# Products and result of an 8x8 forward substitution kept in PSUM (chunked gated delta rule, one Trainium2 core)

## The chip, the cores and the metric

The kernel runs on one core of one Trainium2 chip. The metric is device time in microseconds for one execution. Five engines work side by side, each through its own list of instructions in order, and wait for each other by semaphores: TensorE (PE: matmuls, with its weight loads shown as PEld), VectorE (DVE), ScalarE (ACT), GpSimd (POOL) and SyncE (SP, which here only issues DMAs). On-chip data lie in SBUF, or in PSUM, the eight banks that matmuls write.

## The reference, cut to what matters

One encoder layer in fp32 over 2048 + 256 tokens of width 1024: RMSNorm, one input projection, two mixers side by side (a gated convolution and a bidirectional gated DeltaNet), an output projection, then a mixture of experts and a last RMSNorm. The change lies in the DeltaNet, for which each of 4 heads and each direction solves a unit lower triangular system per chunk of tokens:

```python
lmat = jnp.where(strict, jnp.einsum('bhnid,bhnjd->bhnij', kb, k) * decay, 0.0)
tinv = lax.linalg.triangular_solve(lmat + eye, jnp.broadcast_to(eye, lmat.shape),
                                   left_side=True, lower=True, unit_diagonal=True)
w = jnp.einsum('bhnij,bhnjd->bhnid', tinv, kb * jnp.exp(gc)[..., None])
u = jnp.einsum('bhnij,bhnjd->bhnid', tinv, v * beta[..., None])
...
def step(s, xs):                       # scan over the chunks
    v_new = un - jnp.einsum('bhid,bhde->bhie', wn, s)
    o = jnp.einsum('bhid,bhde->bhie', qd, s) + jnp.einsum('bhij,bhje->bhie', qkn, v_new)
    s = s * jnp.exp(gl)[..., None, None] + jnp.einsum('bhid,bhie->bhde', kd, v_new)
```

## The kernel before, in words

The program is a sequence of stages, each a block of its own: `normalise`, `project` (the input projection, with the convolutions), `decays`, `delta`, `output`, `route`, `experts`, `combine`. Nothing of one stage runs beside the next but what has been issued before.

`delta` goes through 18 chunks of 128 tokens. Chunk `a` is taken forward in lane 0 and backward in lane 1 (`lanes`, one set of tiles `L[d]` and semaphores `E[d]` each), with four heads side by side in every 128x512 tile. `run` writes out the first three and the last three chunks and the step that empties the pipeline, and puts the twelve between them in a loop of two per turn. In the step of chunk `a` the inverse of that chunk is made while the scan of chunk `c` = `a` - 1 is finished. There is no scheduler: every engine's order is the order of the code.

In one step the work follows this chain.

- PE makes k k^T into bank `A[0]` of each lane, DVE multiplies it by the decays (`lt`, L1132), POOL masks out the 8x8 blocks on the diagonal (`near`, L861), DVE folds them (L1135, L1140), and one matmul of PE per step (L990) puts the entries that each row needs for its own block in `local`, which is `L[0]["A"][0]`.
- `solve` on DVE (L1096 to L1111) does the forward substitution for both lanes and all heads at once: seven times a product `step8` = column of `local` times column of `X8` (L1105; one operand in PSUM, one in SBUF, result in SBUF) and a subtraction `X8` - `step8` (L1108 the first, L1110 the rest; both operands in SBUF). Each waits on `base` for the one ahead of it, so there are 14 increments per chunk.
- For each lane DVE spreads `X8` over the block diagonal of `R` by a product with the mask `block8` (L1150; both operands in SBUF) and transposes it into `Tm` (`turn`, L1117).
- Four levels of `inverse` then double the block size, 8 to 128: PE multiplies `M` (POOL's masked parts of `lt`, one per level, L867) by `Tm` into `A[1]` (`X_ready`), ACT copies it to `X` (L945), PE multiplies `X` by `R` into `A[0]` (`dR_ready`), DVE subtracts it from `R` (L1155) and transposes again. At the last level PE transposes (L963) and ACT copies.

PE's order in a step is set in its `step` (L1045 to L1057): the four products of chunk `a`, `s(0)` of the scan, the `local` matmul, `s(1)`, `s(2)`, `s(3)` of the scan (the last is `kdec` by `vn`), then level 0 of `inverse`, whose first matmul waits for `T_set`, the transpose of `R`. POOL's order in a step is `near` for both lanes, `M` of levels 0 and 1, `keT` and `qdT` for both lanes (L876, L877), `M` of levels 2 and 3, then `masked` for the next chunk (L852); each is an operation on 128x512 elements with two operands in SBUF. POOL waits for nothing that `solve` makes.

The lines that the change touches are the allocation of `step8` (L784), the products and subtractions of `solve` (L1105 to L1111) and the operand of L1150.

Of the kernel before, what the change touches and what calls it, by code (L numbers as in the profile page):

```python
# [29 lines left out]
P = 128  # L30
# [6 lines left out]
HEADS = 4  # L37
# [25 lines left out]
def bcast(ap, n, axis):  # L63

    v = ap.unsqueeze(axis)
    shape = list(v.shape)
    shape[axis] = n
    return v.broadcast_to(shape)
# [685 lines left out]
def delta(nc, k, gates, gc_rows, feat, O):  # L754
# [12 lines left out]
    with ExitStack() as ctx:  # L767
        b = Bufs(nc, ctx, "delta_")
        L = []
# [11 lines left out]
            L.append(v)  # L781

        spread = b.sb("spread", [P, 2, HEADS, 8, 8])
        step8, X8 = b.sb("step8", [P, 2 * HEADS, 8]), b.sb("X8", [P, 2 * HEADS, 8])  # L784
        sems = ("loaded0 loaded1 row_loaded0 row_loaded1 masked gates_set kk qk kturned vturned eg_set dec_set lt_set near_set blk_set spread_set qkT_set keT_set "
                "qdT_set M_set kdec_set vtok_set R_set Tturned T_set T_last_set X_ready X_set dR_ready kS_ready rv_set Tv_ready vn_set "
                "o_ready o_added kv_ready S_set").split()
# [1 line left out]
        local_ready, base, begun8 = b.sem("local_ready"), b.sem("base_steps"), b.sem("X8_begun")  # L789
# [2 lines left out]
        NL = LEVELS - BASE  # L792

        local = L[0]["A"][0]

        def tile(d, s):

            if isinstance(s, int) and s >= LT_TILES:
                return s if d == 0 else NT - 1 - (s - LT_TILES)
            return s if d == 0 else s * -1 + (LT_TILES - 1)  # L800
# [261 lines left out]
        def _(dve):  # L1062
            def residual(c, r):
                for d, v, e in lanes:
                    dve.wait_ge(e["vtok_set"], c + 1)
                    dve.wait_ge(e["kS_ready"], c + 1)
                    dve.tensor_tensor(v["rv"][:, :, :], v["vtok"][r][:, :, :], v["B"][0][:, :, :], ALU.subtract).then_inc(e["rv_set"], 1)

            def advance(d, c, r):
                v, e = L[d], E[d]  # L1070
                dve.wait_ge(e["kv_ready"], c + 1)
                dve.wait_ge(e["S_set"], state(c))
                for h in range(HEADS):
                    m = dve.scalar_tensor_tensor(out=v["S"][:, h, :], in0=v["S"][:, h, :], scalar=v["gs"][r][:, 8 + h:9 + h],
                                                 in1=v["B"][1][:, h], op0=ALU.mult, op1=ALU.add)
                m.then_inc(e["S_set"], 1)

            def emit(d, c):

                v, e = L[d], E[d]  # L1080
                dve.wait_ge(e["o_ready"], c + 1)
                wait_if_any(dve, E[1 - d]["o_added"], c)
                out = O[:, bass.ds(tile(d, c), 1), :].rearrange("p a (h c) -> p (a h) c", h=HEADS)
                dve.tensor_tensor(out, v["B"][0][:, :, :], out, ALU.add).then_inc(e["o_added"], 1)

            def clear_state(c):
                for d, v, e in lanes:
                    if c:

                        dve.wait_ge(e["S_set"], c + 1)  # L1090
                    dve.memset(v["S"][:, :, :], 0.0).then_inc(e["S_set"], 1)

            def local_view(d):
                return slice(None, None, -1) if d else slice(None)

            def solve(a):  # L1096

                whole = local[:, :, :].rearrange("p h c -> p (h c)").rearrange("p (m j r) -> p m j r", j=8, r=8)
                unit = k["unit8"][:, :, :]
                dve.wait_ge(local_ready, a + 1)  # L1100
                for j in range(7):
                    w = 7 - j
                    if j:
                        dve.wait_ge(base, a * 14 + 2 * j)
                    dve.tensor_tensor(step8[:, :, 0:w], whole[:, :, j, j + 1:8], bcast(X8[:, :, j], w, 2), ALU.mult).then_inc(base, 1)  # L1105
                    dve.wait_ge(base, a * 14 + (2 * j + 1))
                    if j == 0:
                        dve.tensor_tensor(X8[:, :, 1:8], unit[:, :, 1:8], step8[:, :, 0:w], ALU.subtract).then_inc(base, 1)  # L1108
                    else:
                        dve.tensor_tensor(X8[:, :, j + 1:8], X8[:, :, j + 1:8], step8[:, :, 0:w], ALU.subtract).then_inc(base, 1)  # L1110
                dve.wait_ge(base, a * 14 + 14)  # L1111

            def turn(v, e, r, a, l):

                dve.wait_ge(e["R_set"], a * (NL + 1) + (l + 1))
                flat = [x.rearrange("p h c -> p (h c)") for x in (v["Tm"][:, :, :], v["R"][r][:, :, :])]
                dve.transpose(*flat).then_inc(e["T_set"], 1)  # L1117

            def step(a, c, r):
                if a is None:  # L1120
                    residual(c, 1 - r)
                    for d in range(2):
                        advance(d, c, 1 - r)
                        emit(d, c)
                    return
                if isinstance(c, int) and c == LT_TILES:
                    clear_state(c)
                for d, v, e in lanes:
                    dve.wait_ge(e["dec_set"], a + 1)
                    dve.wait_ge(e["kk"], a + 1)  # L1130
                    wait_if_any(dve, e["M_set"], a * NL)
                    dve.tensor_tensor(v["lt"][:, :, :], v["A"][0][:, :, :], v["dec"][:, :, :], ALU.mult).then_inc(e["lt_set"], 1)  # L1132
                for d, v, e in lanes:
                    dve.wait_ge(e["near_set"], a + 1)
                    dve.tensor_reduce(v["blk"][:, :, local_view(d)], v["near"][:, :, :].rearrange("p h (b r) -> p h r b", r=8),  # L1135
                                      AX.X, ALU.add).then_inc(e["blk_set"], 1)
                    dve.wait_ge(e["blk_set"], a + 1)
                    wait_if_any(dve, local_ready, a)
                    one = k["unit8"][:, d * HEADS:(d + 1) * HEADS, :]
                    dve.tensor_tensor(spread[:, d], bcast(v["blk"][:, :, :], 8, 2), bcast(one, 8, 3), ALU.mult).then_inc(e["spread_set"], 1)  # L1140
                for d, v, e in lanes:
                    dve.wait_ge(e["qk"], a + 1)
                    dve.tensor_tensor(v["qkT"][r][:, :, :], v["A"][1][:, :, :], v["dec"][:, :, :], ALU.mult).then_inc(e["qkT_set"], 1)
                if c is not None:
                    residual(c, 1 - r)
                solve(a)
                for d, v, e in lanes:
                    part = bcast(X8[:, d * HEADS:(d + 1) * HEADS, local_view(d)], P // 8, 2)
                    mask = bcast(k["block8"][:, :].rearrange("p (b r) -> p b r", r=8), HEADS, 1)
                    dve.tensor_tensor(v["R"][r][:, :, :].rearrange("p h (b r) -> p h b r", r=8), part, mask, ALU.mult).then_inc(e["R_set"], 1)  # L1150
                    turn(v, e, r, a, 0)
                for l in range(NL):
                    for d, v, e in lanes:
                        dve.wait_ge(e["dR_ready"], a * NL + (l + 1))
                        dve.tensor_tensor(v["R"][r][:, :, :], v["R"][r][:, :, :], v["A"][0][:, :, :], ALU.subtract).then_inc(e["R_set"], 1)  # L1155
                        if l < NL - 2:
                            turn(v, e, r, a, l + 1)
                    if c is not None and l < 2:
                        advance(l, c, 1 - r)
                        emit(l, c)  # L1160

            clear_state(0)
            dve.tensor_copy(X8[:, :, 0:1], k["unit8"][:, :, 0:1])
            run(dve, step)


# [18 lines left out]
def wait_if_any(eng, sem, value):  # L1185

    if not isinstance(value, int) or value > 0:
        eng.wait_ge(sem, value)
# [901 lines left out]
```

## Time and profile before

| | us |
|---|---|
| time, median of 3 runs (3218.67 to 3228.97) | 3221.87 |
| the profiled execution's own time | 3223.99 |
| its span, first to last instruction | 3222.4 |
| PE busy | 2732.1 (85%) |
| DVE busy | 2039.0 (63%) |
| POOL busy | 1128.5 (35%) |
| ACT busy | 1011.8 (31%) |
| mean granted clock of TensorE, as a share of full speed | 0.924 |

The `delta` stage lies at about 926 to 1671 us of the span. A busy share is a mean over stages with different limits, so the change is read in that stage alone, in a chunk of it. The time of one execution differs from the span by what lies around the span, here 1.6 us.

### The profile page before, as it was taken

The page shows a single profiled execution, that of the slowest core. Times are in us where ns is not written, and L with a number is a line of the kernel's source. Part 1 is how long each engine was busy: PE and PEld are TensorE (multiplying, and loading weights), DVE is VectorE, ACT ScalarE, POOL GpSimd, SP SyncE. Part 2 cuts the span into 40 slices and gives each one's busy share as a digit, 9 for nine tenths or more (in the row PEclk, how much of TensorE's full clock was granted, in tenths as well). Part 3 has the DMA queues.
Part 4 walks back from the last instruction along what each step waited for, and adds up shares of the span by engine and source line. Part 5 has one row for each costly group of instructions (what it writes and reads, how often), then busy time and mean ns, then how long its engine had stood idle before and what let it go on. Part 6 is the DMA issues. An engine that isn't in the chain of part 4 may idle for free. (4 is left out here: it accounts for less than half of the span.)

```text
span 3222.4 us, 45930 instructions
## 1 busy us (share of the span) xinstructions
PE 2732.1 (85%) x15152; PEld 2417.5 (75%) x15153; DVE 2039.0 (63%) x2191; ACT 1011.8 (31%) x2067; POOL 1128.5 (35%) x841
## 2 busy tenths in 40 slices
PE   5999999999858888888888995698899999999840
PEld 4998989989747777777776884576787888778730
DVE  5465564655537777777763335879678576877827
ACT  5152351523523333333323221122222323222223
POOL 4110110101035555555522221444354354435424
PEclk9999999999979999999998997799999999999975
DMA  4011120111121111111005441688567565757639
GB/s 151 27 59 41 48 67 29 58 39 48 42 83 53 53 52 52 52 52 52 27 13 173 138 154 52 240 304 317 205 251 272 208 236 215 286 208 293 235 142 359
DMA packets 228387, 433.96 MB, mean 135 GB/s; under 512 B 15065, under 2 KB 104393, under 8 KB 228170
## 3 DMA queue, kind: packets, MB, share of 16 engines
q1 hardware_dynamic: 207336, 349.86, 31.2%
q0 software_dynamic: 13328, 55.06, 4.7%
q10 hardware_dynamic: 7634, 27.79, 2.1%
q8 instruction: 64, 1.05, 0.1%
q14 instruction: 25, 0.20, 0.0%
HBM read 352.75 MB, written 87.25 MB: 137 GB/s over the span
## 5 line engine op out<-in xcount | busy, mean ns | idle before, releaser
L468 PE MATMUL project_proj<-hT_high,project_w_high 128*128 128x412 f32 (+3 forms) x1392 | 496.3, 357 | 28.0 <-issue 10.4
L468 PE MATMUL project_proj<-hT_low,project_w_high 128*128 128x412 f32 (+3 forms) x1392 | 474.9, 341 | 0.0
L468 PE MATMUL project_proj<-hT_high,project_w_low 128*128 128x412 f32 (+3 forms) x1392 | 474.8, 341 | 0.0
L1682 DVE TENSOR_TENSOR experts_w_low<-experts_w_whole,experts_w_high 128x2048 fp32r<-128x2048 f32 x128 | 355.6, 2778 | 4.4
L1776 PE MATMUL experts_h<-experts_w_high,experts_xT_high 128*128 x848 | 340.5, 401 | 18.8 <-DVE experts_w_low L1682 11.8
L1776 PE MATMUL experts_h<-experts_w_low,experts_xT_high 128*128 x848 | 338.9, 400 | 0.0
L1776 PE MATMUL experts_h<-experts_w_high,experts_xT_low 128*128 x848 | 337.5, 398 | 0.0
L1680 DVE CAST experts_w_high<-experts_w_whole 128x2048 fp32r<-128x2048 f32 x128 | 191.6, 1497 | 168.4 <-DMA experts_w_whole<-in_w_dram 168.3
L468 PEld LDWEIGHTS project_proj<-hT_high,project_w_high 128*128 128x128 f32 (+1 forms) x1392 | 261.4, 188 | 45.1 <-issue 31.6
L958 PE MATMUL delta_prep<-delta_Tm,delta_M 128*128 128x128 f32 x1152 | 185.1, 319 | 119.5 <-DVE delta_Tm L1117 116.9
L468 PEld LDWEIGHTS project_proj<-hT_low,project_w_high 128*128 128x128 f32 (+1 forms) x1392 | 261.3, 188 | 14.4 <-issue 9.8
L468 PEld LDWEIGHTS project_proj<-hT_high,project_w_low 128*128 128x128 f32 (+1 forms) x1392 | 260.9, 187 | 5.2 <-issue 0.7
L958 PEld LDWEIGHTS delta_prep<-delta_Tm,delta_M 128*128 128x128 f32 x1152 | 166.3, 226 | 131.0 <-issue 75.9
L445 POOL CAST project_w_high<-project_w_whole 128x1024 fp32r<-128x1024 f32 x28 | 30.3, 1084 | 639.2 <-DMA project_w_whole<-in_w_tiles_dram 639.2
L1797 PE MATMUL experts_ye<-experts_w_high,experts_gT_high 128*128 128x512 f32 x424 | 178.2, 420 | 55.1 <-DVE experts_w_low L1696 42.1
L1716 POOL COPY experts_ix<-idx 128x1 int32 (+1 forms) x55 | 28.7, 521 | 530.6 <-PE experts_xg_turned L1769 516.6
L1776 PEld LDWEIGHTS experts_h<-experts_w_high,experts_xT_high 128*128 128x128 f32 x848 | 161.3, 190 | 58.5 <-issue 21.3
L945 ACT ACTIVATE delta_X<-delta_prep 128x512 f32<-128x512 f32 x144 | 86.0, 597 | 375.9 <-PE delta_prep L958 375.9
L636 DVE RECIPROCAL project_norms<-project_norms 128x409 f32<-128x409 f32 (+1 forms) x72 | 183.8, 2553 | 24.9 <-ACT project_norms L560 24.4
L1155 DVE TENSOR_TENSOR delta_R<-delta_R,delta_prep 128x512 f32<-128x512 f32 x144 | 97.7, 679 | 160.1 <-PE delta_prep L958 160.1
L867 POOL TENSOR_TENSOR delta_M<-delta_lt,lvl 128x512 f32<-128x512 f32 x144 | 195.2, 1387 | 0.0
L1776 PEld LDWEIGHTS experts_h<-experts_w_low,experts_xT_high 128*128 128x128 f32 x848 | 161.6, 191 | 36.5
(282 smaller groups left out, 5814.3 us busy)
## 6 DMA issues: line engine op xcount, KB each, us to landing
experts_w_whole<-in_w_dram SPq DMA_DIRECT2D x128, 1024.0 KB, 10.1
experts_w_whole<-in_w_dram SPq DMA_DIRECT2D x32, 2048.0 KB, 18.6
delta_qkv<-feat SPq DMA_DIRECT2D x36, 768.0 KB, 4.9
y_rows<-experts_yout ACTq DMA_DIRECT2D x53, 512.0 KB
project_w_whole<-in_w_tiles_dram SPq DMA_DIRECT2D x28, 512.0 KB, 4.3
feat<-project_out SPq DMA_DIRECT2D x48, 205.0 KB, 1.9
normalise_x<-in_x_dram SPq DMA_DIRECT2D x18, 512.0 KB, 3.2
delta_row<-gc_rows SPq DMA_DIRECT2D x36, 256.0 KB, 3.3
```

The lines of the kernel that those rows point to most:

```text
L445: pool.tensor_copy(high[s][:, :, :], whole[s][:, :, :]).then_inc(w_high, 1)
L468: r = pe.matmul(dst, w[s][:, kt, 0:m], x[:, kt, lo:hi], start=kt == 0 and i == 0, stop=kt == KD - 1 and i == 2)
L636: dve.reciprocal(r, r).then_inc(inverted, 1)
L867: pool.tensor_tensor(v["M"][:, l], v["lt"][:, :, :], bcast(k["lvl"][:, d, l, :], HEADS, 1), ALU.mult).then_inc(e["M_set"], 1)
L945: act.activation(v["X"][:, :, :], v["A"][1][:, :, :], ACT.Copy).then_inc(e["X_set"], 1)
L958: m = pe.matmul(out[:, h], lhsT(h), rhs(h), start=start and h == 0, stop=stop, skip_group_check=True)
L1155: dve.tensor_tensor(v["R"][r][:, :, :], v["R"][r][:, :, :], v["A"][0][:, :, :], ALU.subtract).then_inc(e["R_set"], 1)
L1680: dve.tensor_copy(high, loaded).then_inc(e["w_high_set"], 1)
L1682: m = dve.tensor_tensor(low, loaded, high.bitcast(F32), ALU.subtract)
L1716: pool.tensor_copy(ix[p][:, :], idx[:, bass.ds(blk, 1)]).then_inc(e["ix_set"], 1)
L1776: m = pe.matmul(out[:, :], x[p][:, kt, :], w, start=kt == 0 and i == 0, stop=kt == KD - 1 and i == 2)
L1797: m = pe.matmul(Y[n][:, :], g[:, c, :], w, start=c == 0 and i == 0, stop=c == FF // P - 1 and i == 2)
```

## The change

The product tile `step8` moves from SBUF to PSUM, to the first 64 columns of head 0 of `L[1]["A"][0]`, the bank of lane 1 in which k k^T stood and which its levels write again later. The running solution `X8` stays in SBUF. When the 14 operations are done, one copy on DVE puts it into the first 64 columns of head 1 of the same bank (`solved8`), and L1150 (L1153 in the changed file) reads it there instead of `X8`. The copy has its own increment of `base`, so there are 15 per chunk.

```diff
-        step8, X8 = b.sb("step8", [P, 2 * HEADS, 8]), b.sb("X8", [P, 2 * HEADS, 8])
+        X8 = b.sb("X8", [P, 2 * HEADS, 8])
...
         local = L[0]["A"][0]
+        step8, solved8 = (L[1]["A"][0][:, n, 0:16 * HEADS].rearrange("p (m r) -> p m r", r=8) for n in range(2))
...
                 for j in range(7):
                     w = 7 - j
                     if j:
-                        dve.wait_ge(base, a * 14 + 2 * j)
+                        dve.wait_ge(base, a * 15 + 2 * j)
                     dve.tensor_tensor(step8[:, :, 0:w], whole[:, :, j, j + 1:8], bcast(X8[:, :, j], w, 2), ALU.mult).then_inc(base, 1)
-                    dve.wait_ge(base, a * 14 + (2 * j + 1))
+                    dve.wait_ge(base, a * 15 + (2 * j + 1))
...
-                dve.wait_ge(base, a * 14 + 14)
+                dve.wait_ge(base, a * 15 + 14)
+                dve.tensor_copy(solved8[:, :, :], X8[:, :, :]).then_inc(base, 1)
+                dve.wait_ge(base, a * 15 + 15)
...
-                    part = bcast(X8[:, d * HEADS:(d + 1) * HEADS, local_view(d)], P // 8, 2)
+                    part = bcast(solved8[:, d * HEADS:(d + 1) * HEADS, local_view(d)], P // 8, 2)
```

On DVE, the end of `solve` in a step and what follows stood thus before (`delta_step` is `step8` in SBUF):

```order
L1105 TENSOR_TENSOR delta_step<-delta_prep,delta_X 128x8
L1110 TENSOR_TENSOR delta_X<-delta_X,delta_step 128x8
L1150 TENSOR_TENSOR delta_R_1<-delta_X,block 128x512
L1117 STREAM_TRANSPOSE delta_Tm<-delta_R_1 128x512
L1150 TENSOR_TENSOR delta_R_1<-delta_X,block 128x512
L1117 STREAM_TRANSPOSE delta_Tm<-delta_R_1 128x512
```

In the changed kernel the same place reads as follows (`delta_prep` is any of the PSUM banks `A`):

```order
L1106 TENSOR_TENSOR delta_prep<-delta_prep,delta_X 128x8
L1111 TENSOR_TENSOR delta_X<-delta_X,delta_prep 128x8
L1113 COPY delta_prep<-delta_X 128x64
L1153 TENSOR_TENSOR delta_R_1<-delta_prep,block 128x512
L1120 STREAM_TRANSPOSE delta_Tm<-delta_R_1 128x512
L1153 TENSOR_TENSOR delta_R_1<-delta_prep,block 128x512
L1120 STREAM_TRANSPOSE delta_Tm<-delta_R_1 128x512
```

One COPY of 128x64 comes in behind the last subtraction, once per step. No other instruction moves on DVE, and the orders of PE, POOL, ACT and SP are those of before.

## Rows read from the trace of the kernel before

**Rows 1.** Waits in the delta stage, 930 to 1660 us: total, times, longest.

```profile
PE delta_prep L958 <- DVE delta_Tm L1117: 116.7, 26, 11.0
```

**Rows 2.** Timeline of a chunk in the loop and the next, PE: start, us, instructions, [idle before].

```profile
1316.69 1.95 PE L958 MATMUL delta_scan<-delta_vn,delta_kdec 128*128 128x128 f32 x16
...
1324.80 3.75 PE L958 MATMUL delta_prep<-delta_Tm,delta_M 128*128 128x128 f32 x16 [6.16 <-DVE delta_Tm L1117]
...
1331.39 2.38 PE L958 MATMUL delta_prep<-delta_Tm,delta_M 128*128 128x128 f32 x16
...
1336.35 2.32 PE L958 MATMUL delta_prep<-delta_Tm,delta_M 128*128 128x128 f32 x16
...
1365.74 3.75 PE L958 MATMUL delta_prep<-delta_Tm,delta_M 128*128 128x128 f32 x16 [6.20 <-DVE delta_Tm L1117]
```

**Rows 3.** Timeline of the same chunk, DVE.

```profile
1313.41 0.21 DVE L1105 TENSOR_TENSOR delta_step<-delta_prep,delta_X 128x56 f32<-128x56 f32 x1
1313.66 1.12 DVE L1108 TENSOR_TENSOR delta_X<-unit,delta_step 128x56 f32<-128x56 f32 x1
1314.81 0.21 DVE L1105 TENSOR_TENSOR delta_step<-delta_prep,delta_X 128x48 f32<-128x48 f32 x1
1315.05 0.95 DVE L1110 TENSOR_TENSOR delta_X<-delta_X,delta_step 128x48 f32<-128x48 f32 x1
...
1322.11 1.70 DVE L1150 TENSOR_TENSOR delta_R<-delta_X,block 128x512 f32<-128x512 f32 x1
1323.85 0.71 DVE L1117 STREAM_TRANSPOSE delta_Tm<-delta_R 128x512 f32<-128x512 f32 x1
```

**Rows 4.** Timeline of the same chunk, POOL.

```profile
1314.66 1.28 POOL L876 TENSOR_TENSOR delta_keT<-delta_qkv,delta_eg 128x512 f32<-128x512 f32 x1
1315.88 1.28 POOL L877 TENSOR_TENSOR delta_qdT<-delta_qkv,delta_eg 128x512 f32<-128x512 f32 x1
...
1319.55 5.38 POOL L867 TENSOR_TENSOR delta_M<-delta_lt,lvl 128x512 f32<-128x512 f32 x4
1324.89 2.93 POOL L852 TENSOR_TENSOR delta_masked<-delta_row,neg 128x512 f32<-128x512 f32 x2
1347.67 2.51 POOL L861 TENSOR_TENSOR delta_near<-delta_lt,strict 128x512 f32<-128x512 f32 x2 [19.85 <-DVE delta_lt L1132]
```

**Rows 5.** Groups of DVE instructions by shape: busy us, mean ns, idle before.

```profile
L1155 DVE TENSOR_TENSOR delta_R<-delta_R,delta_prep 128x512 f32<-128x512 f32 x144 | 97.7, 679 | 160.1 <-PE delta_prep L958 160.1
L1105 DVE TENSOR_TENSOR delta_step<-delta_prep,delta_X 128x56 f32<-128x56 f32 x18 | 3.8, 212 | 0.0
L1105 DVE TENSOR_TENSOR delta_step<-delta_prep,delta_X 128x8 f32<-128x8 f32 x18 | 3.1, 173 | 0.6
L1140 DVE TENSOR_TENSOR delta_spread<-delta_blk,unit 128x256 f32<-128x256 f32 x36 | 15.5, 430 | 1.2
```

**Rows 6.** The small copies on DVE, each alone: duration in ns, when, shape.

```profile
L1163 DVE COPY delta_X<-unit x1: 111/111/111, 927.9 to 927.9; 128x8 f32<-128x8 f32 x1
L731 DVE COPY decays_ab_gc<-decays_pg x2: 233/234/234, 922.7 to 923.5; 128x72 f32<-128x72 f32 x2
```

**Rows 7.** Stretches: length, PE, PEld, DVE, ACT, POOL busy, granted clock, DMA share.

```profile
1307.00:1318.64 11.64, 11.64 (x95) 10.55 (x93) 10.66 (x18) 4.35 (x12) 11.64 (x10) 1.00 0.01 3
1324.80:1328.13 3.33, 3.33 (x16) 3.33 (x16) 1.39 (x2) 0.60 (x1) 3.03 (x3) 0.50 0.00 0
1290.37:1295.27 4.90, 4.81 (x42) 4.62 (x41) 4.29 (x10) 1.20 (x2) 0.00 (x0) 1.00 0.00 0
```

**Rows 8.** Timeline of a written-out chunk (second of the stage) and of the first.

```profile
996.61 3.78 PE L958 MATMUL delta_prep<-delta_Tm,delta_M 128*128 128x128 f32 x16 [5.89 <-DVE delta_Tm L1117]
1003.46 1.06 PE L958 MATMUL delta_prep<-delta_Tm,delta_M 128*128 128x128 f32 x8
...
955.84 3.78 PE L958 MATMUL delta_prep<-delta_Tm,delta_M 128*128 128x128 f32 x16 [11.04 <-DVE delta_Tm L1117]
...
944.83 0.22 DVE L1105 TENSOR_TENSOR delta_step<-delta_prep,delta_X 128x56 f32<-128x56 f32 x1
```

## The prediction

> **What bounds the kernel now.** I read the waits of the delta stage first, then one chunk of it on PE, DVE and POOL side by side, then the groups for durations and a few stretches for the granted clock. In the waits, PE's longest is for `Tm`, the transposed block diagonal that closes the substitution: 116.7 us in all [rows 1]. The chunk shows where. PE ends the `kdec` by `vn` matmuls of the scan at 1318.64 (1316.69 + 1.95) and then stands idle for 6.16 us until level 0 of the inverse starts at 1324.80 [rows 2]. Before that it had worked without a gap: 11.64 of 11.64 us [rows 7]. What it waits for is one chain on DVE: the substitution starts at 1313.41, the first spread `R` at 1322.11, its transpose ends at 1324.56 (1323.85 + 0.71), and PE follows 0.24 us later [rows 2, 3]. So in this stretch DVE's chain ends last, and its length from 1313.41 to PE's start is 11.39 us.
>
> Why is that chain long? A product of 56 elements with one operand in PSUM takes 0.21 us; a subtraction of 48 elements with both in SBUF takes 0.95, and a `R` of 512 elements with both in SBUF 1.70 [rows 3], where the `R` update of 512 elements with one in PSUM has 0.679 [rows 5]. Size doesn't explain it; POOL does. The subtraction at 1315.05 ends at 1316.00, just behind POOL's `keT` (1314.66 + 1.28 = 1315.94), which started before it; and POOL's operations follow each other every 1.22 us (1314.66 to 1315.88), so each subtraction seems to wait out one of them [rows 3, 4]. A two-operand SBUF instruction that is not held in this way is in the trace too: L1140 has 256 elements in 0.430 [rows 5]. I read this as DVE's second SBUF operand waiting for the POOL instruction that is running.
>
> **The change part by part.** The change leaves one SBUF operand in each instruction of the chain, so I price each as an unheld one.
>
> Seven products write to PSUM instead of SBUF. They go from 212 ns at 56 elements to 173 at 8 [rows 5]; about 0.192 each in the mean, 7 x 0.192 = 1.34 us. The trace has no DVE instruction that writes PSUM. From below, it costs nothing extra; a gain is excluded, since the same elements pass. From above, I let the part of an instruction that does not depend on its size, about 0.165 us (the 8 elements of the 173 ns take few of them: (212 - 173)/48 = 0.8 ns each), come twice. I take nothing, nearest to the row of the same instruction, and keep + 0.165 for the range.
>
> Seven subtractions read `step8` in PSUM and `X8` in SBUF. Nearest is the product itself, the same shape with the same two kinds of operands: again 1.34 us. Now they and the pauses take 8.70 us less these products (1313.41 to 1322.11), so this is where nearly all of the gain lies.
>
> One copy of 64 elements comes in, with its wait: nearest is the copy of 72 elements at 0.233 [rows 6]; from below the copy of 8 at 0.111, from above a held instruction at 0.95 [rows 3]. I take 0.23.
>
> The pauses between dependent instructions stay: 1313.66 - 1313.62 = 0.04 in rows 3, mean about 0.035, for 15 instructions 0.5 us. No increment of `base` moves but the added one, and nothing but `R` is queued behind it.
>
> `R` of the first lane: 0.68 as the 512-element update with one PSUM operand [rows 5], 0.73 with its pause, instead of 1.70. Transpose and PE's reaction stay at 0.71 and 0.24.
>
> Sum from the start of the substitution to PE's level 0: 1.34 + 1.34 + 0.23 + 0.5 + 0.73 + 0.71 + 0.24 = 5.1 us instead of 11.39, so `Tm` comes 6.3 us earlier, at 1318.5. PE is then done with the scan at 1318.64, so its own order ends last and the gain is the idle time, 6.16 us, with next to nothing to spare: whatever the PSUM accesses cost beyond this is paid in full. Twelve chunks in the loop have this pattern. Five of the six written out have 5.89 us of idle time [rows 8]; the first chunk has no scan beside it, so there the chain alone counts: 955.84 - 944.83 = 11.01 less 5.1 is 5.9. Together 12 x 6.16 + 5 x 5.89 + 5.9 = 109.3 us.
>
> A second term hangs on the first. After the idle time the granted clock is 0.50 (1.2 GHz) through the first matmuls of level 0, where it is 1.00 (2.4 GHz) before the idle time and in level 1 of the chunk ahead [rows 7]. Level 0 therefore takes 1331.39 - 1324.80 = 6.59 us to the start of level 1, and level 1 to level 2, the same instructions, 1336.35 - 1331.39 = 4.96 [rows 2]; in the written-out chunks it is 1003.46 - 996.61 = 6.85 [rows 8]. Without the idle time PE comes out of 11 us of gapless work at 1.00, so I count 12 x 1.63 + 5 x 1.89 = 29.0 us. In the first chunk PE still waits 5 us, so I count nothing there.
>
> What is late next: POOL's `M` of level 2. POOL doesn't wait for the substitution, so it makes it at the times of now, from 1319.55, the first two of four by 1322.3 and all by 1324.9 [rows 4]; PE, starting level 0 at 1318.6, asks for level 2 at 1318.6 + 2 x 4.96 = 1328.5. `masked` is done at 1327.8, and the decays that need it come at the end of level 3. POOL then has 19.85 us without work now [rows 4] and would have 12. The second lane's `R` and transpose end 1.4 us behind the first's, at 1319.7, while PE works on the first lane. The other DVE work in the levels has one SBUF operand already, so POOL's shift against it costs nothing.
>
> Against this sum stands the Trainium skill, in "Perfetto Trace Analysis", section "Optimizing Scalar/DVE Operations": about 60 ns of access overhead per DVE operation on SBUF and about 125 on PSUM. Here 56 elements with a PSUM source take 212 ns where L1140's 430 for 256 SBUF elements, less 200 for the difference at 1 ns each ((679 - 430)/256), would make 230: no surcharge for reading. If the page's 65 ns came on top for each of the eight instructions that now write PSUM, an estimate by it is 0.5 us per chunk, 9 us in all.
>
> Total: 109.3 + 29.0 = 138.3 us. From the profiled execution's own 3223.99 this leaves 3085.7; the median of the runs, 3221.87, is 2.1 us lower. I say 3085.
>
> **Rivals.**
>
> *PSUM as a destination costs time.* For it: no row shows such an instruction, and there is no slack. Against: reading PSUM shows no price. With 0.165 more for each of the seven products and the copy, 8 x 0.165 x 18 = 24 us come back: 3109. If instead only the copy is held by POOL like a subtraction now, 0.72 x 18 = 13: 3098. The Trainium skill ("VectorE: DVE Perf Modes", section "Mode 2×_2P — use both read ports for one tensor") has a one-source copy use the second port only with source and destination in SBUF; by that rule the copy isn't held, which takes from this second form.
>
> *The clock doesn't come back.* Level 0 stays at 0.50 for another reason than the idle time. For it: the clock is granted by something that the trace doesn't show. Against: in each chunk it is 1.00 up to the idle time. Time: 3085 + 29 = 3114.
>
> *The change doesn't do what it says.* The subtractions are held whatever their operands, and the copy adds 0.27 with its pause, 18 x 0.27 = 5 us, on the chain that ends last: 3229. Against: the products, with one SBUF operand, are never held (173 to 212 ns in the means) while the same POOL instructions run.
>
> *Slower.* PSUM writes of DVE are held themselves, by TensorE's writes into other banks, which fill the whole substitution now. With h for each of eight such instructions, the chain is 5.1 + 8h, and from h = 0.78 the kernel is slower. At h = 1.0, what `R` is held today (1.70 - 0.68), it is 8.0 - 6.3 = 1.7 us per chunk, 31 in all: 3255. Against: DVE reads PSUM beside the same matmuls and shows no hold.
>
> **How the numbers follow.** Forecast 0.67, with 3076 to 3096 as its own range (the 5 us that the runs of before spread downwards; the page's estimate upwards); PSUM destinations 0.15; clock 0.11; no effect 0.04; slower 0.03. The range of 3074 to 3114 takes in the first three. Under 0.3% (10 us) a measurement of this kernel can't be told from no change: faster 0.93, same 0.04, slower 0.03.
>
> **What would show it.** In the changed profile the subtractions are at about 0.17 to 0.21 us and `R` at 0.68 while POOL runs; the copy at 0.23; PE's wait for `Tm` falls from 116.7 us to under 15, most of it in the first chunk; the stretch from level 0 to level 1 is about 5 us at a granted clock of 1.00; chunks follow every 33 us, where level 0 now starts every 41 (1324.80 to 1365.74) [rows 2]. It is wrong if the products or the copy grow past 0.3 us, if PE still waits more than 1 us per chunk before level 0, or if another wait, `M` of level 2 above all, stands in the levels.

## The result, and the profile after

| | before | changed |
|---|---|---|
| first set of runs, median | 3220.27 us (4 runs, 3217.71 to 3228.97) | 3073.8 us (4 runs, 3070.73 to 3075.78) |
| second set, median | 3218.46 us (14 runs, 3208.05 to 3226.68) | 3075.66 us (5 runs, 3071.51 to 3080.87) |
| ratio, first set | | 0.954 [0.9519, 0.956] |
| ratio, second set | | 0.955 [0.953, 0.9569] |
| profiled execution, and its span | 3223.99, 3222.4 | 3070.73, 3069.1 |
| first `masked` to last `kdec` matmul, in the profile | 930.2 to 1681.4: 751.2 | 922.4 to 1529.8: 607.4 |

The kernel is 4.5% faster. The forecast was 3085, its range 3074 to 3114: the first median lies 0.2 us under the range's low end, the second 1.7 us inside. On which side of the end a median falls is within the scatter of the runs; that the forecast was 9 to 11 us too high is not. The stage `delta` runs to 1681 us in the profile before, ten more than the 1671 given ahead of the prediction.

The wait that bounded the stage, in the waits of the changed kernel (930 to 1540 us; total, times, longest), against [rows 1]:

```profile
PE delta_prep L959 <- DVE delta_Tm L1120: 6.5, 5, 5.0
```

It fell from 116.7 us to 6.5, of which 5.0 are the first chunk's. A chunk of the loop on PE, and level 0 of the next, against [rows 2]:

```profile
1237.47 1.95 PE L959 MATMUL delta_scan<-delta_vn,delta_kdec 128*128 128x128 f32 x16
...
1239.32 2.29 PE L959 MATMUL delta_prep<-delta_Tm,delta_M 128*128 128x128 f32 x16
...
1244.19 2.32 PE L959 MATMUL delta_prep<-delta_Tm,delta_M 128*128 128x128 f32 x16
...
1249.09 2.32 PE L959 MATMUL delta_prep<-delta_Tm,delta_M 128*128 128x128 f32 x16
...
1272.19 2.29 PE L959 MATMUL delta_prep<-delta_Tm,delta_M 128*128 128x128 f32 x16
```

Level 0 starts at 1239.32, where the modelled end of the scan's matmuls is 1239.42: no idle time is left. Level 0 to level 1 takes 4.87 us in place of 6.59, and the next chunk's level 0 comes 32.9 us later in place of 40.9. The same chunk on DVE, against [rows 3]:

```profile
1234.20 0.21 DVE L1106 TENSOR_TENSOR delta_prep<-delta_prep,delta_X 128x56 f32<-128x56 f32 x1
1234.45 0.21 DVE L1109 TENSOR_TENSOR delta_X<-unit,delta_prep 128x56 f32<-128x56 f32 x1
1234.69 0.22 DVE L1106 TENSOR_TENSOR delta_prep<-delta_prep,delta_X 128x48 f32<-128x48 f32 x1
1234.94 0.20 DVE L1111 TENSOR_TENSOR delta_X<-delta_X,delta_prep 128x48 f32<-128x48 f32 x1
...
1237.38 0.23 DVE L1113 COPY delta_prep<-delta_X 128x64 f32<-128x64 f32 x1
1237.64 0.69 DVE L1153 TENSOR_TENSOR delta_R<-delta_prep,block 128x512 f32<-128x512 f32 x1
1238.37 0.71 DVE L1120 STREAM_TRANSPOSE delta_Tm<-delta_R 128x512 f32<-128x512 f32 x1
```

The first subtraction went from 1.12 us to 0.21, `R` from 1.70 to 0.69. From the first product to level 0 it is 5.12 us in place of 11.39. POOL did not get out of the way: it works without a pause from 1227.57 to 1247.79. Rows of it in the same chunk, against [rows 4]:

```profile
1235.45 1.27 POOL L877 TENSOR_TENSOR delta_keT<-delta_qkv,delta_eg 128x512 f32<-128x512 f32 x1
...
1240.38 4.95 POOL L868 TENSOR_TENSOR delta_M<-delta_lt,lvl 128x512 f32<-128x512 f32 x4
1245.30 2.49 POOL L853 TENSOR_TENSOR delta_masked<-delta_row,neg 128x512 f32<-128x512 f32 x2
1260.41 2.51 POOL L862 TENSOR_TENSOR delta_near<-delta_lt,strict 128x512 f32<-128x512 f32 x2 [12.62 <-DVE delta_lt L1135]
```

Its four `M` of levels 2 and 3 even run a little faster (4.95 us in place of 5.38), since DVE's `R` no longer comes between. The groups of the chain, against [rows 5, 6]:

```profile
L1153 DVE TENSOR_TENSOR delta_R<-delta_prep,block 128x512 f32<-128x512 f32 x36 | 24.2, 672 | 0.6
L1113 DVE COPY delta_prep<-delta_X 128x64 f32<-128x64 f32 x18 | 4.1, 228 | 0.6
L1106 DVE TENSOR_TENSOR delta_prep<-delta_prep,delta_X 128x56 f32<-128x56 f32 x18 | 3.9, 215 | 0.0
L1106 DVE TENSOR_TENSOR delta_prep<-delta_prep,delta_X 128x8 f32<-128x8 f32 x18 | 3.1, 174 | 0.6
L1111 DVE TENSOR_TENSOR delta_X<-delta_X,delta_prep 128x48 f32<-128x48 f32 x18 | 3.7, 204 | 0.6
```

Every duration of the sum came out within 12 ns: products 215 to 174 (212 to 173 with SBUF as destination), subtractions 204 at 48 elements, copy 228, `R` 672. The granted clock through the first matmuls of level 0 (third number from the end, 1.00), against the 0.50 of [rows 7]:

```profile
1239.32:1242.65 3.33, 3.33 (x28) 3.14 (x28) 1.15 (x3) 1.19 (x2) 3.33 (x3) 1.00 1.01 280
```

### The profile page after: what moved, and what is told of

The parts are those of the page before. It is cut to its first block and busy times, and to the rows that moved or that the text cites. A ratio compares the mean times of both kernels' runs of the same rounds, so it can differ in the third digit from the quotient of the medians.

```text
span 3069.1 us, 45960 instructions
## 1 busy us (share of the span) xinstructions
PE 2689.6 (88%) x15152; PEld 2375.8 (77%) x15153; DVE 1919.5 (63%) x2209; ACT 1011.7 (33%) x2067; POOL 1105.3 (36%) x841
## 5 line engine op out<-in xcount | busy, mean ns | idle before, releaser
L1685 DVE TENSOR_TENSOR experts_w_low<-experts_w_whole,experts_w_high 128x2048 fp32r<-128x2048 f32 x128 | 349.3, 2729 | 4.4
L468 PEld LDWEIGHTS project_proj<-hT_high,project_w_high 128*128 128x128 f32 (+1 forms) x1392 | 260.5, 187 | 44.3 <-issue 30.4
L868 POOL TENSOR_TENSOR delta_M<-delta_lt,lvl 128x512 f32<-128x512 f32 x144 | 187.3, 1331 | 0.0
L1779 PEld LDWEIGHTS experts_h<-experts_w_high,experts_xT_low 128*128 128x128 f32 x848 | 160.0, 189 | 35.0
L1699 DVE TENSOR_TENSOR experts_w_low<-experts_w_whole,experts_w_high 128x2048 fp32r<-128x2048 f32 x64 | 175.9, 2748 | 2.2
L1800 PE MATMUL experts_ye<-experts_w_low,experts_gT_high 128*128 x424 | 176.4, 416 | 0.0
```

Of the source, the lines that this page charges most:

```text
L468: r = pe.matmul(dst, w[s][:, kt, 0:m], x[:, kt, lo:hi], start=kt == 0 and i == 0, stop=kt == KD - 1 and i == 2)
L868: pool.tensor_tensor(v["M"][:, l], v["lt"][:, :, :], bcast(k["lvl"][:, d, l, :], HEADS, 1), ALU.mult).then_inc(e["M_set"], 1)
L1685: m = dve.tensor_tensor(low, loaded, high.bitcast(F32), ALU.subtract)
L1699: m = dve.tensor_tensor(w2_low[:, p, cs], w2_whole[:, p, cs], w2_high[:, cs].bitcast(F32), ALU.subtract)
L1779: m = pe.matmul(out[:, :], x[p][:, kt, :], w, start=kt == 0 and i == 0, stop=kt == KD - 1 and i == 2)
L1800: m = pe.matmul(Y[n][:, :], g[:, c, :], w, start=c == 0 and i == 0, stop=c == FF // P - 1 and i == 2)
```

## The experiments

Two things were open: that POOL's running instruction, and nothing else about two SBUF operands, made the subtractions slow; and that the clock at level 0 came back because PE's idle time went. Three more questions were how the gain divides, whether there is slack, and what the 8 us are by which the stages ahead of `delta` ended earlier in the profile.

**The changed kernel again.**

> The changed kernel once more, timed against the kernel before in five rounds. Theory A (a DVE instruction with two SBUF operands waits out the POOL instruction that is running; with the operands in PSUM the chain of the substitution is short, and PE's own order comes next): the delta stage, from the first masked of POOL to the last kdec matmul, takes 606 us again, 144 less than before, and the time is 3069 to 3076. The rest of the gain of the first execution, about 8 us by which the stages ahead of delta ended earlier, is then a matter of the single execution: the last matmul of the projection, at 908.4 us in the first profile of before and at 900.7 in that of the changed kernel, comes anywhere between 898 and 911. Rival: the changed program makes the earlier stages faster every time; then the projection ends near 901 again and the ratio stays at or under 0.954.

Measured 3075.66 us, `delta` 608.0 us (928.6 to 1536.6), projection's last matmul at 906.7. Over the eleven profiles of this study that matmul, in code that no kernel here alters, came between 900.7 and 908.4, in no order with the change. The span outside `delta` was 2471.2 us both before and in this execution, and 2461.7 in the first of the changed kernel. So the gain of the change is the 143 to 144 us of `delta`; the rival falls. Why the stages outside `delta` differ by some us from one execution to the next stays open.

**Products in PSUM alone.** No copy, `R` from `X8` (the edit is shown against the changed kernel):

```diff
-                dve.wait_ge(base, a * 15 + 14)
-                dve.tensor_copy(solved8[:, :, :], X8[:, :, :]).then_inc(base, 1)
-                dve.wait_ge(base, a * 15 + 15)
+                dve.wait_ge(base, a * 14 + 14)
...
-                    part = bcast(solved8[:, d * HEADS:(d + 1) * HEADS, local_view(d)], P // 8, 2)
+                    part = bcast(X8[:, d * HEADS:(d + 1) * HEADS, local_view(d)], P // 8, 2)
```

> Products in PSUM, so that the subtractions have one SBUF operand; no copy, and R is made from X8 in SBUF as before (two SBUF operands). Theory A: the subtractions take 0.17 to 0.21 us, R of the first lane is held by whatever POOL runs, 0.7 to 1.7 us, on average some 0.5 above 0.68, against 0.26 saved on the copy. PE waits 0.1 to 0.7 us per chunk for Tm, the granted clock at level 0 is 1.00, time 3074 to 3086. Rival (the copy and R in PSUM carry much of the gain, or the clock drops again): PE waits 1 us or more per chunk, time above 3095.

Measured 3085.74 us, ratio 0.9582 [0.9562, 0.9602]; `delta` 616.9 us, 9 more than the changed kernel. DVE and POOL in a chunk:

```profile
1249.67 1.10 DVE L1151 TENSOR_TENSOR delta_R<-delta_X,block 128x512 f32<-128x512 f32 x1
...
1251.44 1.01 DVE L1151 TENSOR_TENSOR delta_R<-delta_X,block 128x512 f32<-128x512 f32 x1
```

```profile
1248.95 1.27 POOL L878 TENSOR_TENSOR delta_qdT<-delta_qkv,delta_eg 128x512 f32<-128x512 f32 x1
1250.18 1.72 POOL L877 TENSOR_TENSOR delta_keT<-delta_qkv,delta_eg 128x512 f32<-128x512 f32 x1
```

`R` is held until POOL's `qdT` ends at 1250.22, and then 0.55 us remain; POOL's `keT`, which starts beside it, takes 1.72 us in place of 1.27. The hold goes both ways. In the loop level 0 starts about 0.14 us later behind the `local` matmul than in the repeat, and lasts 5.23 us in place of 4.87, since PE waits 0.36 us in it for the second lane's `Tm`; these make up most of the 9 us that the copy and `R` in PSUM are worth of the 143.

**Copy and `R` in PSUM alone.** Products in SBUF as before, the copy and the changed L1150 kept.

> Products in SBUF as before, so the subtractions keep two SBUF operands; only the copy to PSUM is added and R reads it there. Theory A: subtractions 0.93 to 1.1 us as before, copy 0.23, R 0.67 in place of 1.70 in the first lane. The chain is 11.39 - 1.02 + 0.26 = 10.6 us, PE still waits about 5.4 us per chunk, and the granted clock at level 0 is still 0.50; 18 x 0.77 = 14 us gained, time about 3207 (3202 to 3212). Rival (half the gain or more is R's, or the clock comes back once the wait is a little shorter): under 3180.

Measured 3206.53 us, ratio 0.9965 [0.9952, 0.9977], `delta` 738.2 us, 13 less than before. Its level 0, on PE:

```profile
1313.67 3.75 PE L959 MATMUL delta_prep<-delta_Tm,delta_M 128*128 128x128 f32 x16 [5.44 <-DVE delta_Tm L1120]
```

The wait is 0.7 us shorter, and the first matmuls last 3.75 us, as at the low clock before. As expected; the gain is the subtractions', with the clock that follows from them.

**POOL's instructions made short.** The kernel before with `M`, `keT` and `qdT` made for one head of four (the others are zero); the `masked` for the next chunk stay whole. The edit of `M`, with `keT` and `qdT` likewise:

```diff
-                        pool.tensor_tensor(v["M"][:, l], v["lt"][:, :, :], bcast(k["lvl"][:, d, l, :], HEADS, 1),
+                        pool.tensor_tensor(v["M"][:, l, 0:1], v["lt"][:, 0:1, :], bcast(k["lvl"][:, d, l, :], 1, 1),
```

> The kernel before, with POOL's M, keT and qdT made for one of the four heads only (the other three stay zero), so that POOL's instructions beside the substitution have 128 elements instead of 512, some 0.35 to 0.45 us each instead of 1.27. DVE's instructions are those of before, all with two SBUF operands where they had them. Theory A: a subtraction waits out a shorter POOL instruction, so it takes 0.2 to 0.45 us instead of 0.95 while POOL still runs, and 0.17 to 0.21 once POOL has finished its M; the substitution takes 3.2 to 5 us instead of 8.7. Rival (two SBUF operands are slow by themselves, whatever POOL does): the subtractions stay at 0.93 to 1.1 us and the substitution at 8.7.

One substitution ran through all three states of POOL. POOL, then DVE:

```profile
1220.06 1.69 POOL L867 TENSOR_TENSOR delta_M<-delta_lt,lvl 128x128 f32<-128x128 f32 x4
1221.71 2.49 POOL L852 TENSOR_TENSOR delta_masked<-delta_row,neg 128x512 f32<-128x512 f32 x2
```

```profile
1220.67 0.33 DVE L1113 TENSOR_TENSOR delta_X<-unit,delta_step 128x56 f32<-128x56 f32 x1
...
1221.28 0.54 DVE L1115 TENSOR_TENSOR delta_X<-delta_X,delta_step 128x48 f32<-128x48 f32 x1
...
1222.09 0.95 DVE L1115 TENSOR_TENSOR delta_X<-delta_X,delta_step 128x40 f32<-128x40 f32 x1
...
1223.30 0.96 DVE L1115 TENSOR_TENSOR delta_X<-delta_X,delta_step 128x32 f32<-128x32 f32 x1
...
1224.51 0.18 DVE L1115 TENSOR_TENSOR delta_X<-delta_X,delta_step 128x24 f32<-128x24 f32 x1
...
1225.56 0.69 DVE L1155 TENSOR_TENSOR delta_R<-delta_X,block 128x512 f32<-128x512 f32 x1
```

Beside POOL's 128-element `M`, one every 0.41 us, the subtractions take 0.33 and 0.54 us; beside the two 512-element `masked`, 0.95 and 0.96; after POOL's last ends at 1224.20, 0.18, with both operands in SBUF as ever; and `R`, both operands in SBUF too, takes 0.69 us in place of 1.70. This settles the cause: not the operands' place by itself, but POOL's running instruction. The 512-element ones were the `masked`, which I had not counted on, so the values above 0.45 and the 5.13 us of the whole substitution were outside the expectation. The time of this one run, 3074.14 us, is no measure of the gain: `delta` took 634.8 us, 27 more than in the repeat, and the rest of the span 2437.7 us, 33 less than before; the later stages work on other values there, and why they end sooner is not shown.

**The copy five times.**

> The changed kernel with the copy made five times in a row, each waiting for the one ahead: four more of 0.265 us with their pauses on the chain, 1.06 us per chunk. Theory A with no slack left, as the prediction has it: PE waits about 1 us longer per chunk, 18 x 1.06 = 19 us, time about 3091 (3087 to 3094), clock at level 0 still 1.00. Rival (the chain ends well before PE's own order, so there is slack): under 3080. A third way: the longer wait lets the granted clock fall at level 0; then 1.6 to 1.9 us per chunk more, about 3120.

Measured 3098.79 us, ratio 0.9624 [0.9601, 0.9646]; `delta` 627.2 us, 19.2 more than in the repeat of the changed kernel. PE waits 0.95 us per chunk, and the matmuls of level 0 are at full clock:

```profile
1221.53 2.29 PE L959 MATMUL delta_prep<-delta_Tm,delta_M 128*128 128x128 f32 x16 [0.95 <-DVE delta_Tm L1121]
```

In the twelve chunks of the loop the four added copies delay level 0 by 1.05 us, all of what they take, so there the chain on DVE still ends last, without slack; in the five written out behind the first chunk they delay it by 0.84 to 0.91, so there PE's own order had ended some 0.2 us behind the chain. From the `local` matmul to level 0 the changed kernel takes 6.31 us in the loop and 6.22 in four of those five; an estimate from these is that shortening the chain further could still give about 0.1 us per chunk of the loop, 1 us in all. The median lies 5 us above the expectation's upper end, where the stage in the profile has the expected 19; the runs go from 3093.87 to 3105.32.

**PE kept busy, substitution as before.** Filling matmuls (identity by identity, into a bank that is free there) ahead of level 0, first 40, then 20, then 28:

```diff
                 s(3)
+                for d, v, e in lanes:
+                    pe.wait_ge(e["qkT_set"], a + 1)
+                for n in range(10):          # then 5, then 7
+                    by_heads(L[1]["A"][1], lambda h: k["ident"][:, :], lambda h: k["ident"][:, :])
                 for l in range(NL):
```

> The kernel before, with 40 matmuls of 128 columns (identity by identity, into a bank that is free there) put on PE behind the scan's kdec matmuls and ahead of level 0: about 4.6 us of the 6.16 us in which PE waits for Tm. The substitution is left as it was. Theory A with the second term of the prediction (the clock falls because PE is idle): the chain on DVE still ends last, PE waits some 1.5 us, the granted clock at level 0 is 1.00, level 0 to level 1 takes 4.9 us instead of 6.59, and 17 x 1.6 to 1.9 = 28 to 31 us are gained, time about 3190 (3186 to 3196). Rival (the low clock at level 0 has another reason): no gain, 3215 to 3225, granted clock 0.50 there.

Measured 3227.52 us, ratio 1.0027 [1.0017, 1.0037]: no gain, and `delta` 8.5 us longer. That was my sizing: each fp32 matmul is recorded as two instructions, so the filling took 8.9 us and delayed level 0. The time therefore decides nothing between the theories. The trace does: with no idle time left ahead of level 0, the clock there is 1.00 in all 17 chunks behind the first, and level 0 takes 4.53 us, with the substitution as slow as before.

> The kernel before with half as many filling matmuls on PE as in the run before it: 20 of 128 columns. In that run 40 were recorded as 80 instructions of 0.11 us each (fp32 takes two), 8.9 us from start to start in place of 4.6, so PE reached level 0 about 2.8 us after Tm was there, though the granted clock was 1.00 and level 0 to level 1 took 4.53 us. With 20 the filling takes 4.5 us of the 6.3 that PE waits. Theory A (the clock at level 0 follows from PE's idle time): PE waits about 1.6 us for Tm, clock 1.00 at level 0, level 0 to level 1 4.9 us in place of 6.59; 12 x 1.7 + 5 x 1.9 = 30 us gained, time about 3189 (3184 to 3194). Rival (what the changed kernel gained at level 0 came from the shorter R and transposes of the second lane and not from the clock): gain under 10 us.

Measured 3212.6 us, ratio 0.9966 [0.9951, 0.9982], `delta` 8.5 us shorter. The clock did not stay up throughout. Two chunks on PE, the first with the clock at 1.00, the second where it fell:

```profile
1273.85 1.13 PE L958 MATMUL delta_prep<-delta_Tm,delta_M 128*128 128x128 f32 x8 [1.71 <-DVE delta_Tm L1121]
1275.34 1.16 PE L958 MATMUL delta_prep<-delta_Tm,delta_M 128*128 128x128 f32 x8 [0.35 <-DVE delta_Tm L1121]
1279.07 2.32 PE L958 MATMUL delta_prep<-delta_Tm,delta_M 128*128 128x128 f32 x16
...
1313.43 1.13 PE L958 MATMUL delta_prep<-delta_Tm,delta_M 128*128 128x128 f32 x8 [1.72 <-DVE delta_Tm L1121]
1314.92 1.97 PE L958 MATMUL delta_prep<-delta_Tm,delta_M 128*128 128x128 f32 x8 [0.36 <-DVE delta_Tm L1121]
1320.22 1.01 PE L958 MATMUL delta_prep<-delta_Tm,delta_M 128*128 128x128 f32 x7
```

Level 0 to level 1 is 5.22 us in the first and 6.79 in the second; of the 17 chunks behind the first, 9 were of the second kind, with the same waits as the others (1.4 to 1.8 us, and 0.3 to 0.5 in the second lane's half). My expectation of 30 us failed.

> The kernel before with 28 filling matmuls on PE, between the 20 and the 40 of the two runs ahead of this one: 56 instructions of 0.1115 us are 6.2 us, which closes the 6.3 us that PE waits for Tm to about 0.1. With 20 it still waited 1.7 us and the clock fell all the same in 9 of 17 chunks, in the second lane's half of level 0. Theory A: with no idle time left the clock is 1.00 in level 0 of all chunks, level 0 to level 1 takes 5.2 us (6.59 before; the 0.35 that the changed kernel saves beyond this is the second lane's shorter R), the chain on DVE is not touched, so 17 x 1.4 = 24 us are gained, time 3192 to 3202. Rival: the clock falls in some chunks also without idle time, gain under 15 us.

Measured 3200.52 us, ratio 0.9937 [0.9923, 0.995], 20 us less than before, and 23.5 us less in `delta` of the profile (727.8). No chunk behind the first fell. Level 0 in one of them, on PE and in the clock:

```profile
1304.19 6.42 PE L958 MATMUL delta_prep<-ident 128*128 128x128 f32 x56
1310.55 1.13 PE L958 MATMUL delta_prep<-delta_Tm,delta_M 128*128 128x128 f32 x8
1312.04 1.16 PE L958 MATMUL delta_prep<-delta_Tm,delta_M 128*128 128x128 f32 x8 [0.36 <-DVE delta_Tm L1121]
...
1315.78 1.54 PE L958 MATMUL delta_prep<-delta_Tm,delta_M 128*128 128x128 f32 x9
```

```profile
1310.57:1315.80 5.23, 4.87 (x42) 4.68 (x42) 3.02 (x5) 1.20 (x2) 3.02 (x3) 1.00 0.00 0
```

With the substitution untouched and as slow as ever, level 0 takes 5.23 us in place of 6.6. The second term is real, and it hangs on PE's idle time.

> The kernel before with 20 filling matmuls as two runs ahead, but on data (kdec by kdec) in place of identity by identity, which is nearly all zeros. If the clock fell in 9 of 17 chunks there because of the 1.7 us that PE still waits, it falls in about as many here. Rival: it fell because multiplying zeros counts for less; then it is 1.00 in all chunks here and level 0 to level 1 takes 5.2 us in each.

One run, 3211.88 us: with data in place of zeros the clock fell in 11 of the 17 chunks. So zeros were not the reason.

## Why the prediction was right in its steps and short in its size

The mechanism held: the hold by POOL, its end, the return of the clock. What failed is the size, in two places: three terms of the sum were about 5 us too small together, and the base from which the sum was taken was about 4 us too high. Both erred the same way.

- *The hold by POOL, and its end with one operand in PSUM*: right, and shown by the run with POOL's short instructions. One reading beside it was not: L1140, taken as an instruction that is not held, had started ahead of POOL's and held POOL instead (its rows are in the last section).
- *PSUM as a destination costs nothing*: right but for a little. The seven products sum to 1.39 us in the repeat's profile where they took 1.345, 6 ns each. The estimate by "Perfetto Trace Analysis" of the Trainium skill, section "Optimizing Scalar/DVE Operations", 65 ns each, is ten times what the trace shows, and the measurement decides. As a source PSUM costs nothing that shows either: `R` took 672 ns from PSUM, and 670 with both operands in SBUF in the run with POOL's short instructions. The copy was not held (228 ns). That agrees with "VectorE: DVE Perf Modes" of the Trainium skill, section "Mode 2×_2P — use both read ports for one tensor", by which a copy uses both read ports only on SBUF; which ports this copy used, no run shows.
- *"the gain is the idle time, 6.16 us"*: mis-sized by 2 us. The profile's idle time starts at the modelled end of the last matmul; back to back, PE starts the next one ahead of that end (in the chunk above 1237.47 + 1.95 = 1239.42, and level 0 starts at 1239.32). The time given back is read from start to start. From the `local` matmul to level 0 the twelve loop chunks went from 12.56 to 6.31 us, the five written out from 12.38 to 6.31, the first from 12.14 to 6.01: 75.0 + 30.4 + 6.1 = 111.5 us against 109.3. That PE's own order would end last was not so in the loop, by about 0.1 us (the run with five copies).
- *The clock term, 29.0 us*: 12 x 1.76 + 5 x 1.92 = 30.8 measured, from level 0 to level 1. Its size was near, partly by luck, since its account was not whole: the fill of 28 shows 5.23 us at full clock with the slow substitution, the changed kernel 4.87, so about 0.36 us per chunk, 6 us in all, come from the second lane's shorter `R` and the rest from the clock. The first chunk did keep its low clock, with 6.57 us in the repeat and 6.00 in the first profile of the changed kernel, after 6.67.
- The levels behind level 0 were put at no change. Level 1 to level 2 went from 4.96 to 4.90 us in 17 chunks: 1 us.
- Together 143.3 us against 138.3, with 143.2 measured in `delta` of the repeat: the sum was 5 us short, by these three terms.
- *"From the profiled execution's own 3223.99 this leaves 3085.7; the median of the runs, 3221.87, is 2.1 us lower. I say 3085."* This step missed the rest, and it is the largest single one. The sum was taken from one profiled execution, which lay high: the medians of the four later sets of before are 3218.46, 3218.91, 3221.45 and 3220.47, and that of all 61 runs is 3219.7, 4.3 us lower. From 3219.7 less 143.2 one gets 3076.5, and the nine runs of the changed kernel, 3070.73 to 3080.87, have their median at 3075.24. A low end of 3074 left 11 us for a sum that was 5 short, a base that was 4 high and runs that scatter by 5 to either side.
- *What is late next*: nothing was. `M` of level 2 is there at 1243 (half of the four from 1240.38), PE asks for it at 1249.09.

## What to carry to other kernels

When a small VectorE instruction takes as long as whatever GpSimd runs beside it, look at where its operands lie: one of two moved to PSUM ended the hold here, for 8 us per chunk on a chain that PE waited for. Size a removed wait from start to start, not by the idle column, and add what the idle time did to the granted clock. Subtract the sum from the median of many runs and not from the one that was profiled, and let the range take in their scatter on the side to which the sum leans.

## What the runs showed of the hardware that was not expected

The clock's fall is not a fixed price of a given idle time. Counted over the 17 chunks behind the first, by the idle time ahead of level 0: after 5.9 to 6.2 us (before) and 5.1 to 5.4 (copy and `R` alone) level 0 began at the low level in every one; after 1.4 to 1.8 us, with 0.3 to 0.5 more inside level 0, the clock fell in 9 (11 in the run on data); after at most 1.6 us in 2, in the run with POOL's short instructions; after 0.7 to 1.0 us, with five copies, in none. Nor does a fall always cost the same: after the same 5.4 us of idle time, level 0 to level 1 took between 5.98 and 7.40 us in the chunks of the run with the copy and `R` alone. What decides between these cases stays open.

The hold between VectorE and GpSimd goes both ways: GpSimd's 1.27 us became 1.72 where VectorE's `R` had been let in. The kernel before shows it too, in the instruction that the prediction took as not held, L1140 with both operands in SBUF. It starts 0.03 us ahead of POOL's first `M`, and it is `M` that takes 1.53 us in place of 1.28:

```profile
1309.21 0.42 DVE L1140 TENSOR_TENSOR delta_spread<-delta_blk,unit 128x256 f32<-128x256 f32 x1
...
1309.24 1.53 POOL L867 TENSOR_TENSOR delta_M<-delta_lt,lvl 128x512 f32<-128x512 f32 x1
```

In these rows the instruction that started first ran at its own pace, and the other waited.
